# Expert jobs of 100 token slots instead of 128, and room for five overflow jobs, in a two-layer hybrid decoder trunk

## The chip, the cores and the metric

The kernel runs on one core of a Trainium2 chip. The metric is the device time of one execution in microseconds. Engines are named as in the profile: PE is the matrix engine and PEld its weight loads, DVE, ACT and POOL are the vector, scalar and general engines, SP is the engine that issues most DMAs. A matmul has a stationary operand, which is loaded into the array first, and a moving operand, whose columns stream through it.

## What is computed

The reference is a trunk of two layers on 256 tokens of width 1024, in float32. Each layer has a mixer (mLSTM heads and stick-breaking attention between one input and one output projection) and a channel mixer: a dense SwiGLU in layer 0, and in layer 1 eight experts of which every token takes two. The change concerns the experts:

```python
def _moe_swiglu(h, w_router, w_gate, w_up, w_down):
    logits = (h @ w_router).astype(jnp.float32)
    top_val, top_idx = lax.top_k(logits, TOP_K)           # TOP_K = 2, N_EXPERTS = 8
    top_w = jax.nn.softmax(top_val, axis=-1)
    combine = jnp.sum(jax.nn.one_hot(top_idx, N_EXPERTS) * top_w[..., None], axis=-2)
    out = jnp.zeros_like(h)
    for e in range(N_EXPERTS):
        out = out + combine[..., e:e + 1] * _swiglu(h, w_gate[e], w_up[e], w_down[e])
    return out
```

An expert's SwiGLU is `(silu(h @ w_gate) * (h @ w_up)) @ w_down`, with `w_gate` and `w_up` of 1024 x 3584 and `w_down` of 3584 x 1024. 256 tokens with two choices each make 512 pairs of token and expert, 64 for an expert on average. With the reference's own draw of inputs its router gives the eight experts 64, 79, 52, 85, 48, 84, 54 and 46 tokens.

## The kernel before

**Weights.** All weights stream from HBM in pieces of 1 MB (128 partitions x 2048 float32), through six buffers `raw`. Each piece is split on the chip into a high part `whi` (ACT, line 709) and a low part `wlo` (DVE, line 1169), with three buffers each. The products of float32 operands are made of three passes on PE (`passes`, line 1754): high x high, low activation x high weight, high activation x low weight. A piece takes 12 matmuls.

**Semaphores along a piece.** SP loads piece i when DVE has split piece i-6 (`lo_ready`); ACT splits piece i when PE has used piece i-3 (`piece_used`); DVE follows ACT; PE waits for `lo_ready`.

**Expert jobs.** A job is one expert on up to 128 tokens, in slots. It has 42 pieces: for each of seven blocks of 512 hidden columns two pieces of `w_gate`, two of `w_up` and two of `w_down`. In a job the tokens are the stationary operand (128 x 128: 128 features by 128 slots) and the weights move (512 columns). `product` makes gate and up into PSUM rows by slot, ACT and DVE form silu x up (lines 1052 and 1621), `hid_transpose` (line 2290) turns the 128 x 512 result in four transposes, ACT and DVE split it (lines 1058 and 1615), and `down_piece_job` multiplies with `w_down`. Eight jobs follow each other without a pause in PE's order: the next job's rows are fetched from `x_by_slot` by slot, turned in eight transposes (`gather`, line 2253) and split (lines 1040 and 1608) before the last down block of the job at hand. At the job's end ACT copies the result rows (line 1083) and sends them to `o_by_slot`. The first job gathers with matmuls against a one-hot matrix of slots (line 2240), the last adds its rows with a scatter matrix (lines 2324 to 2330), and the rows of the first seven are fetched back by an indirect gather (line 684) and added in the last job (line 1674).

**Overflow jobs.** Where an expert has more than 128 tokens, the rest goes to an overflow job, of which there may be `EXTRA = 3`. `count_extras` on DVE (the `ovf` lines in the diff) marks such experts and scans the marks; POOL makes from them a table with the expert of each overflow job and the count of all jobs (lines 666 to 679), in a chain of small operations, each waiting for the one before. At the end every engine loads the count and runs a loop of `EXTRA` rounds whose body is skipped when there is no such job (`Fori(E, JOBS)` and `If(j < jobs)`, on DVE lines 1730 to 1732, on PE lines 2373 to 2375).

**Routing, ahead of the jobs.** DVE makes the one-hot slots (line 1579) and the position of each token, POOL the rows for the indirect stores into `x_by_slot` (lines 615 to 630).

Of the kernel before, what the change touches and what calls it, by code (L numbers as in the profile page):

```python
# [63 lines left out]
EXTRA = 3  # L64
# [27 lines left out]
DUMP = E * P  # L92


def trunk(nc, x, w_in, b_igate, b_fgate, conv_w, conv_b, g_mlstm, g_sb, w_out,
# [4 lines left out]
    o_by_slot = nc.dram_tensor("o_by_slot", ((E - 1) * P, D), F32, kind="Internal").ap()  # L100
    with ExitStack() as ctx:
# [70 lines left out]
        table = sb("table", [P, 4])  # L172
        table_i = sb("table_i", [1, 4], I32)
# [42 lines left out]
        def first_rows(k):  # L216
            return ps[:, GATHER_BANK[k // 2], P * (k % 2):P * (k % 2 + 1)]
# [144 lines left out]
        def _(sp):  # L362
# [91 lines left out]
            def job(e, next_rows=False):  # L454
# [5 lines left out]
                for f in range(EB):  # L460
# [23 lines left out]
            jobs = sp.value_load(table_i[0:1, 3:4], min_val=E, max_val=JOBS)  # L484
# [18 lines left out]
        def _(pool):  # L503
# [82 lines left out]
            for e in range(1, E):  # L586
                pool.dma_start(x_by_slot[e * P:(e + 1) * P, :], vs[:].rearrange("p t d -> p (t d)")
                               ).then_inc(zero_rows, 16)
# [26 lines left out]
            routing_op(pool.tensor_scalar(where[:, 3, 0], iota_e[:], float(P), -1.0, ALU.mult, ALU.add))  # L615
            routing_op(pool.tensor_scalar(v, job_pos[:, :, 0:E], float(P), None, ALU.is_le))
# [46 lines left out]
            made, upto = ovf[:, 0], ovf[:, 1]  # L663
# [29 lines left out]
        def _(act):  # L693
# [342 lines left out]
            def gathered(o):  # L1036

                for half in range(2):
                    act.wait_ge(xg_ps, loop.at("half", 2 * o + half + 1))
                    act.activation(xT_hi[:, 4 * half:4 * half + 4, 0:P],  # L1040
                                   ps[:, 2 + half, :].rearrange("p (c t) -> p c t", t=P),
                                   ACT.Copy).then_inc(xg_hi_ready, 1)

            def scatter_matrix():
                act.wait_ge(scatT_ps, loop.at("job", 2 - E))
                act.activation(scatT[:], ps[:, 6, 0:256].rearrange("p (t c) -> p t c", t=TT),
                               ACT.Copy).then_inc(scatT_ready, 1)

            def e_silu(i, f):

                act.wait_ge(piece_used, loop.at("piece", n + i + 1))
                act.activation(silu[:, 0:512], ps[:, 2 * (f % 2), :], ACT.Silu).then_inc(e_sil, 1)

            def hid_high(f):
                act.wait_ge(e_hidT, loop.at("block", f + 1))
                if f >= 2:
                    act.wait_ge(piece_used, loop.at("piece", n + down_piece(f - 2, 1, EB) + 1))
                act.activation(hid_hi[:, f % 2, 0:512], ps[:, 4 + f % 2, :], ACT.Copy
                               ).then_inc(e_hid_hi, 1)
# [1365 lines left out]
```

## Time and profile before

| | |
|---|---|
| median of 3 runs | 1419.68 us (1419.65 to 1420.23) |
| profiled execution, its own time | 1420.34 us |
| its span | 1418.5 us |
| first matmul of the expert stage | 455.36 us |
| last weight matmul | 1406.56 us |

The span is that of the recorded instructions; the device time holds some 1.8 us around it. Matmuls overlap in the trace: each is shown with its whole passage through the array, and the next starts long before that ends. So the time that a matmul costs is read from the distance between starts. In the trace the three passes are named by their operands, moving first (`whi,xT_hi`, `whi,xT_lo`, `wlo,xT_hi`), and `128*100 128x256` means a stationary operand of 128 rows and 100 columns and a moving one of 256 columns.

### The profile page before, as it was taken

Reading aid. Unit: us, or ns where it says so; the run is one execution under the profiler, and the core shown is the slowest. Engines: PE = TensorE matmul, PEld = TensorE weight load, DVE = VectorE, ACT = ScalarE, POOL = GpSimd, SP = SyncE. Lnnn points to the kernel's source line nnn. Section 1 sums busy time; section 2 is a strip of 40 time slices with the busy share of each in tenths; the row PEclk is TensorE's granted clock in tenths of the full one; section 3 lists DMA queues with packets and bytes.
Section 4 is the critical chain, followed back from the end, with each engine's and each line's share of the span. In section 5 each row is a group of like instructions: output and inputs, shape, how many; then the busy total and the mean of one; then the engine's idle time right before and its main releaser. Section 6 shows DMA issues by size and latency. Waiting matters only on the chain.

```text
span 1418.5 us, 19026 instructions
## 1 busy us (share of the span) xinstructions
PE 1406.9 (99%) x7007; PEld 1185.5 (84%) x7007; DVE 1141.0 (80%) x854; ACT 1006.3 (71%) x866; POOL 161.4 (11%) x195
## 2 busy tenths in 40 slices
PE   9999999999999999999999999999999999999997
PEld 9988888889988888888888888888888888888885
DVE  6677554457587888888898988888888898888997
ACT  6877533445887777777777777777777777777775
POOL 2210000000101999500000000000000000002000
PEclk9999999999999999999999999999999999999999
DMA  9845655564544899999999999999999999999993
GB/s 352 268 153 191 215 198 178 176 195 152 183 149 144 325 394 397 392 395 385 364 383 393 370 380 392 382 369 390 382 361 385 392 370 380 382 389 376 394 394 135
DMA packets 188546, 447.04 MB, mean 315 GB/s; under 512 B 7736, under 2 KB 9920, under 8 KB 188496
## 3 DMA queue, kind: packets, MB, share of 16 engines
q1 hardware_dynamic: 184048, 431.12, 83.3%
q0 software_dynamic: 3440, 11.58, 2.2%
q10 hardware_dynamic: 1008, 3.67, 0.6%
q8 instruction: 32, 0.52, 0.2%
q14 instruction: 18, 0.15, 0.0%
HBM read 435.84 MB, written 10.49 MB: 315 GB/s over the span
## 4 chain that ended last, share of the span: by engine, by line
PE 97%; DVE 1%; ACT 1%; issue 0%; DMA 0%; SPq 0%; DVEq 0%; ACTq 0%
PE ps L1754 90%; PE ps L2290 2%; PE ps L2253 0%; PE ps L1786 0%; PE ps L1989 0%; PE ps L2113 0%; PE ps L1878 0%; DMA raw<-in_w_in_dram 0%; PE ps L2240 0%; ACT whi L709 0%; PE ps L1942 0%; PE ps L1775 0%; PE ps L1880 0%; DVE ssc L1380 0%; DVE y L1393 0%
## 5 line engine op out<-in xcount | busy, mean ns | idle before, releaser
L1169 DVE TENSOR_TENSOR wlo<-raw,whi 128x2048 fp32r<-128x2048 f32 x401 | 917.9, 2293 | 209.0 <-ACT whi L709 207.6
L709 ACT ACTIVATE whi<-raw 128x2048 fp32r<-128x2048 f32 x402 | 771.3, 1919 | 345.6 <-PE ps L1754 339.4
L1754 PE MATMUL ps<-whi,xT_hi 128*128 128x512 f32 (+1 forms) x1232 | 485.9, 394 | 0.3
L1754 PE MATMUL ps<-wlo,xT_hi 128*128 128x512 f32 (+1 forms) x1232 | 479.7, 389 | 0.0
L1754 PE MATMUL ps<-whi,xT_lo 128*128 128x512 f32 (+1 forms) x1232 | 478.8, 389 | 0.0
L1754 PEld LDWEIGHTS ps<-wlo,xT_hi 128*128 128x128 f32 x1232 | 231.2, 188 | 48.7
L1754 PEld LDWEIGHTS ps<-whi,xT_hi 128*128 128x128 f32 x1232 | 231.4, 188 | 46.6 <-issue 1.1
L1754 PEld LDWEIGHTS ps<-whi,xT_lo 128*128 128x128 f32 x1232 | 231.6, 188 | 44.9
L1754 PE MATMUL ps<-whi,hid_hi 128*128 128x512 f32 x536 | 210.2, 392 | 0.0
L1754 PE MATMUL ps<-wlo,hid_hi 128*128 128x512 f32 x536 | 208.8, 390 | 0.0
L1754 PE MATMUL ps<-whi,hid_lo 128*128 128x512 f32 x536 | 208.7, 389 | 0.0
L1754 PEld LDWEIGHTS ps<-wlo,hid_hi 128*128 128x128 f32 x536 | 100.6, 188 | 21.0
L1754 PEld LDWEIGHTS ps<-whi,hid_hi 128*128 128x128 f32 x536 | 100.7, 188 | 20.3
L1754 PEld LDWEIGHTS ps<-whi,hid_lo 128*128 128x128 f32 x536 | 100.7, 188 | 20.3
L684 POOL DMA_INDIRECT qsT<-o_by_slot,slot_out x1 | 1.8, 1792 | 707.9 <-DMA o_by_slot<-vm 707.9
L1754 PE MATMUL ps<-xT_hi,whi 128*128 128x256 f32 x252 | 72.3, 287 | 1.0 <-DVE wlo L1251 0.8
L1754 PE MATMUL ps<-xT_lo,whi 128*128 128x256 f32 x252 | 71.2, 283 | 0.0
L1754 PE MATMUL ps<-xT_hi,wlo 128*128 128x256 f32 x252 | 71.2, 283 | 0.0
L1754 PEld LDWEIGHTS ps<-xT_hi,whi 128*128 128x128 f32 x252 | 48.2, 191 | 2.0 <-issue 1.7
L1754 PEld LDWEIGHTS ps<-xT_lo,whi 128*128 128x128 f32 x252 | 48.3, 192 | 0.0
L1754 PEld LDWEIGHTS ps<-xT_hi,wlo 128*128 128x128 f32 x252 | 48.2, 191 | 0.0
L719 ACT ACT_TABLE_LOAD x32 | 41.1, 1283 | 1.3 <-PEq L2400 0.8
(286 smaller groups left out, 904.8 us busy)
## 6 DMA issues: line engine op xcount, KB each, us to landing
raw<-in_moe_w_gate_dram SPq DMA_DIRECT2D x112, 1024.0 KB, 7.2
raw<-in_moe_w_up_dram SPq DMA_DIRECT2D x112, 1024.0 KB, 7.3
raw<-in_moe_w_down_dram SPq DMA_DIRECT2D x112, 1024.0 KB, 7.3
raw<-in_w_in_dram SPq DMA_DIRECT2D x25, 1024.0 KB, 5.6
raw<-in_ffn_w_gate_dram SPq DMA_DIRECT2D x10, 1024.0 KB, 5.0
raw<-in_ffn_w_up_dram SPq DMA_DIRECT2D x10, 1024.0 KB, 5.1
raw<-in_ffn_w_down_dram SPq DMA_DIRECT2D x10, 1024.0 KB, 4.9
raw<-in_w_out_dram SPq DMA_DIRECT2D x8, 1024.0 KB, 5.1
```

Source lines behind the costliest of these rows:

```text
L684: pool.indirect_dma_start(picked[t][c], None, o_by_slot, bass.IndirectOffsetOnAxis(ap=slot_out[:, t, c:c + 1], axis=0)).then_inc(picked_in ...
L709: act.activation(whi[:, i % NSPLIT, :], raw[:, i % NRAW, :], ACT.Copy).then_inc(hi_ready, 1)
L719: act.preload_act_table_set(name)
L1169: dve.tensor_tensor(wlo[:, i % NSPLIT, :], raw[:, i % NRAW, :], whi[:, i % NSPLIT, :].bitcast(F32), ALU.subtract).then_inc(lo_ready, 1)
L1754: ins = pe.matmul(acc, lhs, rhs, start=start and m == 0, stop=stop and m == 2, skip_group_check=True)
L2290: ins = pe.transpose(ps[:, 4 + f % 2, k * P:(k + 1) * P], prod[:, k * P:(k + 1) * P], ident[:])
```

## The change

A job holds `SLOTS = 100` tokens instead of 128. Every operand of a job that had 128 slots has 100: the stationary operands of the products (`xT_hi`, `xT_lo`, `hid_hi`, `hid_lo`) have 100 columns, PSUM results and their evacuations that lie by slot in the partitions use 100 partitions, those that lie by slot in the free dimension are read as four groups of 100 columns out of 128 (`slot_columns`). The transposes read 100 rows and write 100 columns. `x_by_slot` and `o_by_slot` have 100 rows for each expert. An expert has one overflow job above 100 tokens and a second above 200; there may be five such jobs, so the skipped loops have five rounds. DVE counts them with one operation more, and POOL finds the expert of each by a range test in place of an equality, with two operations more for each overflow job and one ahead of them.

```diff
-EXTRA = 3
+SLOTS = 100
+EXTRA = 5
...
-DUMP = E * P
+DUMP = E * SLOTS
...
         def first_rows(k):
-            return ps[:, GATHER_BANK[k // 2], P * (k % 2):P * (k % 2 + 1)]
+            return ps[:, GATHER_BANK[k // 2], P * (k % 2):P * (k % 2) + SLOTS]
+
+        def slot_columns(v):
+
+            return v.rearrange("p (c t) -> p c t", t=P)[:, :, 0:SLOTS]
...
                         sp.wait_ge(xg_ps, loop.at("half", 2))
-                        sp.dma_start(x_slots, x_by_slot[bass.ds((e + 1) * P, P), :]
+                        sp.dma_start(x_slots[0:SLOTS], x_by_slot[bass.ds((e + 1) * SLOTS, SLOTS), :]
                                      ).then_inc(x_slots_in, 16)
...
+            table_op(pool.tensor_tensor(before, upto, before, ALU.subtract))
             for r in range(EXTRA):
-                table_op(pool.tensor_scalar(of, upto, float(r + 1), None, ALU.is_equal))
-                table_op(pool.tensor_tensor(of, of, made, ALU.mult))
+                table_op(pool.tensor_scalar(of, upto, float(r + 1), None, ALU.is_ge))
+                table_op(pool.tensor_scalar(names, before, float(r), None, ALU.is_le))
+                table_op(pool.tensor_tensor(of, of, names, ALU.mult))
                 table_op(pool.tensor_tensor(names, of, iota_e[:], ALU.mult))
                 sum_of(table[:, r:r + 1], names)
-                table_op(pool.tensor_scalar(back, of, -float(P), None, ALU.mult))
+                table_op(pool.tensor_scalar(back, before, float(SLOTS), -float((r + 1) * SLOTS),
+                                            ALU.mult, ALU.add))
+                table_op(pool.tensor_tensor(back, back, of, ALU.mult))
...
             def e_silu(i, f):
 
                 act.wait_ge(piece_used, loop.at("piece", n + i + 1))
-                act.activation(silu[:, 0:512], ps[:, 2 * (f % 2), :], ACT.Silu).then_inc(e_sil, 1)
+                act.activation(silu[0:SLOTS, 0:512], ps[0:SLOTS, 2 * (f % 2), :], ACT.Silu
+                               ).then_inc(e_sil, 1)
...
-                            act.activation(o_rows[:, c, :], ps[:, 6 + c, :], ACT.Copy
+                            act.activation(o_rows[0:SLOTS, c, :], ps[0:SLOTS, 6 + c, :], ACT.Copy
                                            ).then_inc((o_copied, o_free)[c], 1)
...
             def hid_low(f):
                 dve.wait_ge(e_hid_hi, loop.at("block", f + 1))
-                dve.tensor_tensor(hid_lo[:, f % 2, 0:512], ps[:, 4 + f % 2, :],
-                                  hid_hi[:, f % 2, 0:512].bitcast(F32), ALU.subtract
+                dve.tensor_tensor(slot_columns(hid_lo[:, f % 2, 0:512]), slot_columns(ps[:, 4 + f % 2, :]),
+                                  slot_columns(hid_hi[:, f % 2, 0:512].bitcast(F32)), ALU.subtract
                                   ).then_inc(e_hid, 1)
...
             def count_extras():
 
-                own(dve.tensor_scalar(ovf[:, 0], ps[:, 7, 16:24], float(P), None, ALU.is_gt))
+                own(dve.tensor_scalar(ovf[:, 2], ps[:, 7, 16:24], float(SLOTS), None, ALU.is_gt))
+                own(dve.scalar_tensor_tensor(ovf[:, 0], ps[:, 7, 16:24], float(2 * SLOTS), ovf[:, 2],
+                                             ALU.is_gt, ALU.add))
...
-                        ins = pe.transpose(ps[:, 2 + c // 4, P * (c % 4):P * (c % 4) + P],
-                                           x_slots[:, c * P:(c + 1) * P], ident[:])
+                        ins = pe.transpose(ps[:, 2 + c // 4, P * (c % 4):P * (c % 4) + SLOTS],
+                                           x_slots[0:SLOTS, c * P:(c + 1) * P],
+                                           ident[0:SLOTS, 0:SLOTS])
...
-                        ins = passes(ps[:, bank, :], xT_hi[:, kk, 0:P], xT_lo[:, kk, 0:P],
+                        ins = passes(ps[0:SLOTS, bank, :], xT_hi[:, kk, 0:SLOTS], xT_lo[:, kk, 0:SLOTS],
                                      hi[:, k, :], lo[:, k, :], start=half == 0 and k == 0,
                                      stop=half == 1 and k == 3, weights_move=True)
...
                 for k in range(4):
-                    ins = pe.transpose(ps[:, 4 + f % 2, k * P:(k + 1) * P],
-                                       prod[:, k * P:(k + 1) * P], ident[:])
+                    ins = pe.transpose(ps[:, 4 + f % 2, k * P:k * P + SLOTS],
+                                       prod[0:SLOTS, k * P:(k + 1) * P], ident[0:SLOTS, 0:SLOTS])
...
-                    hs = slice((2 * half + kk) * P, (2 * half + kk + 1) * P)
+                    hs = slice((2 * half + kk) * P, (2 * half + kk) * P + SLOTS)
                     s = slice(c * 512, (c + 1) * 512)
-                    ins = passes(ps[:, 6 + c, :], hid_hi[:, f % 2, hs], hid_lo[:, f % 2, hs],
+                    ins = passes(ps[0:SLOTS, 6 + c, :], hid_hi[:, f % 2, hs], hid_lo[:, f % 2, hs],
                                  hi[:, kk, s], lo[:, kk, s],
```

The other operands by slot are cut in the same way: the first gather and its copies, the splits of the gathered rows, the product, the scatter matrix, the last rows and their scatter.

## Rows read from the trace of the kernel before

**Rows 1.** The page, busy time of each engine.
```profile
PE 1406.9 (99%) x7007; PEld 1185.5 (84%) x7007; DVE 1141.0 (80%) x854; ACT 1006.3 (71%) x866; POOL 161.4 (11%) x195
```
**Rows 2.** Windows: us, busy by engine, PEclk, DMA share, GB/s; one job, then the stage.
```profile
808.39:926.92 118.53, 118.53 (x541) 98.14 (x540) 105.13 (x59) 89.37 (x60) 0.00 (x0) 1.00 1.02 380
...
459.05:1406.56 947.51, 947.51 (x4316) 784.31 (x4314) 842.84 (x486) 710.25 (x480) 128.85 (x134) 1.00 1.01 375
```
**Rows 3.** Waits from 573 to 1284 us: us in total, times, longest. The answer has five rows.
```profile
ACT whi L709 <- PE ps L1754: 164.1, 235, 0.9
DVE wlo L1169 <- ACT whi L709: 80.3, 192, 1.3
...
PEld ps L1754 <- DVE wlo L1169: 0.2, 1, 0.2
```
**Rows 4.** Timeline of PE, expert stage: start us, us, matmul; first and last of 12 distances.
```profile
799.75 0.39 PE L1754 MATMUL ps<-whi,xT_hi 128*128 128x512 f32 x1
...
802.47 0.39 PE L1754 MATMUL ps<-whi,hid_hi 128*128 128x512 f32 x1
```
**Rows 5.** Timeline of PEld, the same stretch.
```profile
800.20 0.19 PEld L1754 LDWEIGHTS ps<-whi,xT_hi 128*128 128x128 f32 x1
800.43 0.19 PEld L1754 LDWEIGHTS ps<-whi,xT_lo 128*128 128x128 f32 x1
```
**Rows 6.** Timeline of PE, mixer, 256 moving columns; first and last of 12 distances.
```profile
55.77 0.28 PE L1754 MATMUL ps<-xT_lo,whi 128*128 128x256 f32 x1
...
57.21 0.28 PE L1754 MATMUL ps<-xT_lo,whi 128*128 128x256 f32 x1
```
**Rows 7.** Timeline of PE, 384 moving columns; first and last of 7 distances.
```profile
293.93 0.33 PE L1754 MATMUL ps<-whi,xT_hi 128*128 128x384 f32 x1
...
295.14 0.33 PE L1754 MATMUL ps<-whi,xT_lo 128*128 128x384 f32 x1
```
**Rows 8.** Timeline of PE, gate products, 100 stationary columns; first and last of 14 distances.
```profile
24.61 0.28 PE L1942 MATMUL ps<-xT_lo,wif_hl 128*100 128x256 f32 x1
...
26.25 0.28 PE L1942 MATMUL ps<-xT_lo,wif_hl 128*100 128x256 f32 x1
```
**Rows 9.** Groups of PEld by form: busy us, mean ns, idle before.
```profile
L1754 PEld LDWEIGHTS ps<-whi,xT_hi 128*128 128x128 f32 x1232 | 231.4, 188 | 46.6 <-issue 1.1
...
L1942 PEld LDWEIGHTS ps<-xT_hi,wif_hl 128*100 128x100 f32 x16 | 2.7, 166 | 0.0
```
**Rows 10.** The chain, 800 to 830 us: start us, us, what.
```profile
808.55 0.87 PE ps L2253 x8
```
**Rows 11.** Timeline of ACT, DVE and PE from the end of one job into the next.
```profile
814.92 1.92 ACT L709 ACTIVATE whi<-raw 128x2048 fp32r<-128x2048 f32 x1 [0.80 <-PE ps L1754]
816.75 1.06 ACT L1083 ACTIVATE vm<-ps 128x512 f32<-128x512 f32 x2
818.43 3.85 ACT L709 ACTIVATE whi<-raw 128x2048 fp32r<-128x2048 f32 x2 [0.63 <-ACT vm L1083]
820.38 4.50 DVE L1169 TENSOR_TENSOR wlo<-raw,whi 128x2048 fp32r<-128x2048 f32 x2 [1.22 <-ACT whi L709]
822.89 0.40 PE L1754 MATMUL ps<-whi,xT_hi 128*128 128x512 f32 x1
```
**Rows 12.** The page, DMA issues: KB each, median us to landing.
```profile
raw<-in_moe_w_gate_dram SPq DMA_DIRECT2D x112, 1024.0 KB, 7.2
```
**Rows 13.** POOL: window of the table (us, busy), and its wait behind it.
```profile
514.48:590.29 75.81, 69.78 (x77) 1.00 1.04 395
POOL qsT L684 <- DMA o_by_slot<-vm: 707.9, 1, 707.9
```
**Rows 14.** DVE's skipped loop, by line: duration ns min/median/max, first and last start.
```profile
L1732 DVEq COMPARE_BRANCH  x3: 63/63/69, 1402.3 to 1404.1; - x3
L1731 DVEq COMPARE_BRANCH  x3: 50/66/72, 1403.0 to 1404.4; - x3
```
**Rows 15.** The end: chain (start us, us, what) and PE's skipped loop by line.
```profile
1406.25 0.70 DVE hid_lo L1627
...
1414.19 0.66 DVEq L101
L2375 PEldq COMPARE_BRANCH  x3: 221/221/3725, 1408.7 to 1413.8; - x3
```

More of the change, by code:

```diff
@@ L171, in trunk @@
         ovf = sb("ovf", [P, 8, E])
-        table = sb("table", [P, 4])
-        table_i = sb("table_i", [1, 4], I32)
+        table = sb("table", [P, EXTRA + 1])
+        table_i = sb("table_i", [1, EXTRA + 1], I32)
         slot_in = sb("slot_in", [P, TT, 2], I32)
@@ L483, in _ @@
             sp.wait_ge(table_ready, 1)
-            jobs = sp.value_load(table_i[0:1, 3:4], min_val=E, max_val=JOBS)
+            jobs = sp.value_load(table_i[0:1, EXTRA:EXTRA + 1], min_val=E, max_val=JOBS)
             with sp.Fori(E, JOBS) as j:
@@ L614, in _ @@
             pool.wait_ge(picked_second, 1)
-            routing_op(pool.tensor_scalar(where[:, 3, 0], iota_e[:], float(P), -1.0, ALU.mult, ALU.add))
-            routing_op(pool.tensor_scalar(v, job_pos[:, :, 0:E], float(P), None, ALU.is_le))
+            routing_op(pool.tensor_scalar(where[:, 3, 0], iota_e[:], float(SLOTS), -1.0, ALU.mult,
+                                          ALU.add))
+            routing_op(pool.tensor_scalar(v, job_pos[:, :, 0:E], float(SLOTS), None, ALU.is_le))
             for t in range(TT):
@@ L1100, in rows_of_job_behind @@
                         act.wait_ge(piece_used, loop.at("piece", n))
-                    act.activation((o_hi, o_plain)[c], ps[:, 6 + c, :], ACT.Copy).then_inc(o_hi_ready, 1)
+                    act.activation((o_hi, o_plain)[c][0:SLOTS], ps[0:SLOTS, 6 + c, :], ACT.Copy
+                                   ).then_inc(o_hi_ready, 1)
             def start_of_job(first=False):
@@ L1108, in start_of_job @@
                             act.wait_ge((xg_first, xg_ps)[k // 2 % 2], k // 4 + 1)
-                        act.activation(xT_hi[:, k, 0:P], first_rows(k), ACT.Copy,
+                        act.activation(xT_hi[:, k, 0:SLOTS], first_rows(k), ACT.Copy,
                                        scale=gT[:, ROUTE_SEAM, k:k + 1]).then_inc(xg_first_hi, 1)
@@ L1125, in _ @@
             act.wait_ge(table_ready, 1)
-            jobs = act.value_load(table_i[0:1, 3:4], min_val=E, max_val=JOBS)
+            jobs = act.value_load(table_i[0:1, EXTRA:EXTRA + 1], min_val=E, max_val=JOBS)
             with act.Fori(E, JOBS) as j:
@@ L1600, in one_hot @@
                         else job_pos[:, t, (0, E - 1)[o]:(1, E)[o]]
-                    dve.tensor_scalar(slots[:, t, :], iota[:], at, None, ALU.is_equal
+                    dve.tensor_scalar(slots[:, t, 0:SLOTS], iota[:, 0:SLOTS], at, None, ALU.is_equal
                                       ).then_inc(slots_ready, 1)
@@ L1729, in _ @@
             dve.wait_ge(table_ready, 1)
-            jobs = dve.value_load(table_i[0:1, 3:4], min_val=E, max_val=JOBS)
+            jobs = dve.value_load(table_i[0:1, EXTRA:EXTRA + 1], min_val=E, max_val=JOBS)
             with dve.Fori(E, JOBS) as j:
@@ L2239, in first_gather @@
                     for c in range(KC):
-                        ins = pe.matmul(first_rows(c), h[:, t, c * P:(c + 1) * P], slots[:, t, :],
+                        ins = pe.matmul(first_rows(c), h[:, t, c * P:(c + 1) * P], slots[:, t, 0:SLOTS],
                                         start=t == 0 and c % 2 == 0, stop=t == 1, skip_group_check=True)
@@ L2263, in scatter_matrix @@
                 for t in range(TT):
-                    ins = pe.transpose(ps[:, 6, t * P:(t + 1) * P], slots[:, t, :], ident[:])
+                    ins = pe.transpose(ps[0:SLOTS, 6, t * P:(t + 1) * P], slots[:, t, 0:SLOTS], ident[:])
                 ins.then_inc(scatT_ps, 1)
@@ L2323, in scatter @@
                     bank = ps[:, 2 + 2 * t, :]
-                    pe.matmul(bank, scatT[:, t, :], o_hi, start=True, stop=False,
+                    pe.matmul(bank, scatT[0:SLOTS, t, :], o_hi[0:SLOTS], start=True, stop=False,
                               skip_group_check=True)
-                    pe.matmul(bank, scatT[:, t, :], o_lo, start=False, stop=True,
+                    pe.matmul(bank, scatT[0:SLOTS, t, :], o_lo[0:SLOTS], start=False, stop=True,
                               skip_group_check=True).then_inc(scat_ps, 1)
@@ L2329, in scatter @@
                 for t in range(TT):
-                    pe.matmul(ps[:, 3 + 2 * t, :], scatT[:, t, :].bitcast(F32), o_plain, start=True,
-                              stop=True, skip_group_check=True).then_inc(scat_ps, 1)
+                    pe.matmul(ps[:, 3 + 2 * t, :], scatT[0:SLOTS, t, :].bitcast(F32), o_plain[0:SLOTS],
+                              start=True, stop=True, skip_group_check=True).then_inc(scat_ps, 1)
             def start_of_job(first=False):
@@ L2372, in _ @@
             pe.wait_ge(table_ready, 1)
-            jobs = pe.value_load(table_i[0:1, 3:4], min_val=E, max_val=JOBS)
+            jobs = pe.value_load(table_i[0:1, EXTRA:EXTRA + 1], min_val=E, max_val=JOBS)
             with pe.Fori(E, JOBS) as j:
```

39 lines of the change are left out of this document (19 added, 20 removed).

## The prediction

> **What bounds the kernel now.** I read the page first: PE is busy for 99% of the span, but a busy share of overlapping matmuls says only that PE is never empty, and DVE is at 80% [rows 1]. So the question is whether PE is fed all the time. The windows show one job of 118.53 us with PE full, DVE busy for 105.1 us (89%) and ACT for 89.4 us, the clock at its full level and 380 GB/s moving; the expert stage is 947.5 us, two thirds of the span [rows 2]. The waits of that stage then tell who is late: ACT waits for PE to free a split buffer (164 us), DVE waits for ACT, and PE waited for DVE once, for 0.2 us [rows 3]. The stage is bound by PE alone, and each nanosecond between two starts of its matmuls counts.
>
> What is that distance? In a product of a job 12 distances take 802.47 - 799.75 = 2.72 us, so 226.7 ns each for 512 moving columns [rows 4]. In the mixer, with the same 128 stationary columns, 12 distances take 1.44 us for 256 moving columns: 120.0 ns [rows 6]; with 384, 7 distances take 1.21 us: 173 ns [rows 7]. From 256 to 512 columns the distance grows by 106.7 ns, 0.417 ns a column, one column per cycle at 2.4 GHz. What is left is the same at all three lengths: 226.7 - 213.3 = 13.4, 173 - 160 = 13, 120.0 - 106.7 = 13.3 ns. So every matmul pays a fixed 13.3 ns that its moving columns do not explain. It isn't the wait for the weight load: the load for the next matmul begins with the present one (800.20, 800.43) and takes 0.19 us, so it is done some 35 ns before the next start [rows 4, 5].
>
> As a check on a job: 8 x 42 pieces x 12 matmuls are 4032 in the stage, 504 in a job. 504 x 0.2267 = 114.3 us. A job has 28 + 8 transposes; eight of them are 0.87 us, 0.109 us each [rows 10], so 36 are 3.9 us. Together 118.2 us of the 118.53 measured [rows 2]. Nothing large is missing.
>
> **The change, part by part.**
>
> *The stationary operand of 4032 matmuls has 100 columns instead of 128.* The trace has one place with this shape: the gate products of the mixer at L1942, in the same number format, with 256 moving columns. Their 14 distances take 26.25 - 24.61 = 1.64 us, 117.1 ns each [rows 8], against 120.0 ns with 128 stationary columns [rows 6]. The fixed part is then 117.1 - 106.7 = 10.4 ns, and 13.3 x 100/128 = 10.4 ns: it goes by the stationary columns, 0.104 ns for each. As the fixed part didn't depend on the moving length, I take the difference of 2.9 ns over to 512 columns: 226.7 becomes 223.8 ns. Rounding of the starts (0.01 us in 14 and in 12) leaves 0.7 to 0.8 ns on each distance, so 2.9 is between some 2 and 4. The sum: 4032 x 2.9 ns = 11.7 us, with 8.1 and 16 us at these ends. The bounds from both sides: no gain if the difference of L1942 has another cause; at most the whole fixed part, 4032 x 13.3 ns = 54 us. I take 11.7 because both rows differ in the stationary columns and in nothing else that I can see. The loads become shorter too, 188 to 166 ns [rows 9]; they lie beside the matmul, so I count that at nothing.
>
> The Trainium skill (TensorE: Matmul & The Clock Gate, section Back-to-back issue gap) gives the warm gap of an isolated matmul as N/2.4 + 2.5 ns, with N the moving columns and no term for the stationary ones; that is an estimate of 216 ns here. The rows have 226.7 ns [rows 4], and two distances at one N that differ by 2.9 ns [rows 6, 8]; by the rule the change would bring nothing from PE, which is the first rival below.
>
> *Transposes and first gather.* In a transpose the data are the stationary operand, with 128 columns as before; only the identity, which moves, shrinks from 128 to 100 columns. Their distance of 109 ns [rows 10] is twice the 53 ns that 128 columns stream, so something else sets it (the load, it seems) and 100 columns bring nothing. The same holds for the first gather. The final scatter keeps 128 stationary and 512 moving columns and has 100 rows instead of 128, which I price at nothing: it is eight matmuls.
>
> *ACT and DVE.* Copies and subtractions that lie by slot in the free dimension have 400 elements per partition instead of 512, and are shorter; those that lie by slot in the partitions still have 512 and should keep their time. None is on PE's path as long as pieces arrive in time. The place with least cover is the seam between jobs. ACT splits a piece (from 814.92), copies the result rows (816.75, two of them), sends them and splits again (818.43, two pieces); DVE follows with the second at 820.38 + 2.29 = 822.67, and PE starts that piece at 822.89 [rows 11]. The cover is 0.22 us. No operation of this chain becomes shorter (splits of 2048, copies of 512 elements), while PE's 36 matmuls of three pieces become 36 x 2.9 ns = 0.10 us shorter. So 0.12 us are left. If that fell short, each seam would pay the shortfall, seven times; if all cover of 0.22 us had to be paid on top, 1.5 us. I put 0.1 us for it, as it is thin.
>
> *Weight DMAs.* A piece of 1 MB lands 7.2 us after its issue [rows 12]. It is issued when DVE has split the piece six before, and needed when ACT starts on it, six pieces of 2.82 us (118.53/42) less 1.92 + 2.29 us later: 12.7 us. That leaves 5.5 us, of which the change takes 0.2. The rate rises from 380 to 380 x 118.5/117.1 = 385 GB/s, and the window of the table shows 395 [rows 13]. Price nothing. The row stores and loads become smaller.
>
> *POOL's table.* The chain had 77 operations in 75.81 us [rows 13], 0.985 us each. It was 25 for each of three jobs and two behind; it becomes 27 for each of five, one ahead and two behind: 138, so 61 more, 60 us. Queued behind it on POOL is the indirect gather of the result rows, which waits 707.9 us for the seventh job's store [rows 13]; the four engines that load the table do so at the end. The cover is ten times the cost. Without it the last job's additions would be late. The one operation more on DVE lies in the first job, where DVE has its 11% of slack [rows 2].
>
> *Skipped loops.* Two rounds more on each engine. On DVE the branches of three rounds run from 1402.3 to 1404.4, 0.7 us a round [rows 14]; two more end at about 1405.8. DVE's next operation starts at 1406.25 [rows 15], released by ACT, which waits for PE: 0.4 us of cover, and nothing to pay. If DVE's rounds were dearer, up to 1.4 us would stand in the path; I put 0.1 us. PE's loop starts at 1408.7 behind its last work and its third round begins at 1413.8, with a first branch of 3.7 us; two rounds at 0.7 us end near 1415.6, after DVE's last work but before the last stores are in, at 1418.5 [rows 15]. ACT waits for PE's last piece at that time, SP for DVE's last rows; both have microseconds.
>
> **Sum.** -11.7 + 0.1 + 0.1 = -11.5 us. The profiled execution took 1420.34 us with a span of 1418.5, so its span would become 1407.0. The median of the runs before is 1419.68 us, 0.7 below the profiled execution, and the difference goes on it: 1419.7 - 11.5 = 1408.2 us.
>
> **Rivals.**
> 1. *The matmuls don't speed up.* The distance at 512 moving columns stays at 226.7 ns, because the 2.9 ns of L1942 belong to short matmuls or to a quieter stretch (only 14 distances in a row). Against it: the fixed part was one value at 256, 384 and 512 [rows 4, 6, 7]. Time: 1419.7 + 0.2 = 1419.9 us, so this is also the case that the change doesn't do anything measurable.
> 2. *PE gains, but the splits hold it back.* At 89% of a job DVE is near to PE, and the seam has 0.12 us. If strided operands made the slot operations longer instead of shorter, so that each seam lost 0.3 us and each of 56 blocks 0.05 us, 7 x 0.3 + 56 x 0.05 = 4.9 us would come back: 1413 us.
> 3. *Slower: a ninth job runs.* It starts with the 101st token of any expert, costs a whole job of 118.5 us and some 10 us of unhidden gather and scatter at both ends, and gives 1408.2 + 128 = 1536 us. Against it: before there were exactly 8 jobs (112 gate pieces, 14 a job) [rows 12], so no expert has over 128, and the largest count of the reference's draw is 85.
> 4. *More than the share.* Loads shorter by 22 ns [rows 9] could relieve PE beyond the fixed part's share; half of the 13.3 ns would be 27 us, 1393 us.
> 5. *Loads become longer.* If loads were on a fast path that only 128 columns have, they would at 100 take perhaps twice as long, 376 ns, and set the distance: +150 ns x 4032 = +600 us, 2020 us. The 166 ns of L1942's loads speak against it [rows 9].
>
> The Trainium skill (TensorE: Matmul & The Clock Gate, section Weight-path perf modes) has such a path: fast weight load is on when the number of weights is 128 and the type isn't FP32. By the loads of 188 and 166 ns, in the proportion of a fixed time and the columns, it isn't in use here.
>
> **Chances.** Forecast 0.76, with 1406.5 to 1410.5 as its own range; rival 1 0.11; rival 2 0.06; rival 3 0.04; rival 4 0.02; rival 5 0.01. A measurement of this kernel tells 0.2% (2.8 us) from no change. Faster: 0.76 + 0.06 + 0.02 = 0.84. Same: 0.11. Slower: 0.05. The range takes in the forecast and rival 2, 0.82 together: 1405.5 to 1414 us.
>
> **What the profile after would show.** Distances of 223.8 ns in the products of a job and a job of 118.53 - 504 x 0.0029 = 117.1 us; loads of 166 ns; transposes still 109 ns apart; no new wait of PE for DVE; 112 gate pieces; POOL's table ending near 650 us; DVE's loop done before 1395 (1405.8 - 11.5 is 1394.3) and its next operation when ACT releases it. Distances of 226.7 ns would prove me wrong at the root; distances of 223.8 with a job of over 117.5 us would show the splits or seams.

## The result and the profile after

| | before | after |
|---|---|---|
| median | 1419.66 us | 1437.26 us |
| span of the profiled execution | 1418.5 us | 1435.9 us |

The changed kernel is slower: the ratio is 1.0123, with a 95% interval of 1.0111 to 1.0135. The forecast was 1408.2 us, faster.

The page of the changed kernel, busy time of the engines and its groups (busy us, mean ns, idle before); compare [rows 1, 9]:

```profile
PE 1424.5 (99%) x7007; PEld 1087.8 (76%) x7007; DVE 1133.3 (79%) x855; ACT 999.0 (70%) x866; POOL 206.6 (14%) x256
...
L1768 PE MATMUL ps<-whi,xT_hi 128*100 128x512 f32 (+2 forms) x1232 | 489.2, 397 | 0.7 <-DVE wlo L1182 0.4
...
L1768 PEld LDWEIGHTS ps<-whi,hid_lo 128*100 128x100 f32 (+1 forms) x536 | 90.3, 168 | 33.1
...
raw<-in_moe_w_gate_dram SPq DMA_DIRECT2D x112, 1024.0 KB, 7.2
```

As many matmuls as before, 112 gate pieces, so eight jobs and no overflow job. PE still has no pause, its loads became shorter, DVE and ACT have less to do, and it takes longer. The windows of one job and of the stage (us, busy of PE, PEld, DVE, ACT, POOL, granted clock, DMA share, GB/s), to be read against [rows 2]:

```profile
815.31:935.97 120.66, 120.66 (x542) 85.85 (x541) 104.11 (x59) 88.48 (x60) 0.00 (x0) 1.00 1.02 372
459.05:1424.19 965.14, 964.76 (x4315) 685.94 (x4314) 834.58 (x486) 702.99 (x480) 174.18 (x195) 1.00 1.00 367
```

A job takes 120.66 us instead of 118.53: 8 x 2.13 = 17.0 of the 17.4 us by which the span grew. The clock is at its full level in both. The timeline of PE from a gate and up product into a down piece (start us, us, matmul), first and last of 20 distances, answers to [rows 4]:

```profile
805.87 0.40 PE L1768 MATMUL ps<-whi,xT_hi 128*100 128x512 f32 x1
...
810.54 0.40 PE L1768 MATMUL ps<-wlo,hid_hi 128*100 128x512 f32 x1
```

4.67 us for 20 distances are 233.5 ns, against 226.7 ns before. The transposes went the other way. The chain of the changed kernel (start us, us, what), against [rows 10]:

```profile
815.47 0.69 PE ps L2267 x8
```

0.086 us each, from 0.109. The two together give the job: before, (118.53 - 36 x 0.109) / 504 = 227.4 ns on average for a product's matmul, some distances being stretched; after, (120.66 - 36 x 0.086) / 504 = 233.3 ns. So the matmuls cost 4032 x 5.9 ns = 23.8 us and the transposes give back 0.023 us each; there are 8 x 28 in the hidden blocks and 7 x 8 in the gathers, as the first job gathers with matmuls, so that is 280 x 0.023 = 6.4 us. The balance is 17.4 us.

The waits of the stage hold a second, small thing (us in total, times, longest):

```profile
ACT whi L721 <- DMA raw<-in_moe_w_gate_dram: 3.3, 2, 2.5
...
PEld ps L1768 <- DVE wlo L1182: 1.1, 2, 0.8
```

ACT waited for weight DMAs, which before it didn't, in the stretch of [rows 3] or in the rest of the stage, and PE once for its split, for 0.55 us beyond a normal distance.

### The profile page after: what moved, and what is told of

It is laid out like the page before. It is cut to its first block, busy times and chain, and to the rows that moved or that the text cites. A ratio compares the mean times of both kernels' runs of the same rounds, so it can differ in the third digit from the quotient of the medians.

```text
span 1435.9 us, 19120 instructions
## 1 busy us (share of the span) xinstructions
PE 1424.5 (99%) x7007; PEld 1087.8 (76%) x7007; DVE 1133.3 (79%) x855; ACT 999.0 (70%) x866; POOL 206.6 (14%) x256
## 4 chain that ended last, share of the span: by engine, by line
PE 94%; DVE 2%; DMA 2%; ACT 1%; issue 1%; SPq 0%; DVEq 0%; ACTq 0%
PE ps L1768 88%; PE ps L2305 1%; DMA raw<-in_moe_w_gate_dram 1%; DMA h<-in_x_dram 1%; ACT whi L721 1%; DVE wlo L1182 1%; PE ps L1800 0%; PE ps L2003 0%; PE ps L2127 0%; PE ps L2267 0%; PE ps L1892 0%; ACT y L746 0%; PE ps L2254 0%; SPq L412 0%; PE ps L1789 0%
## 5 line engine op out<-in xcount | busy, mean ns | idle before, releaser
L1768 PE MATMUL ps<-whi,xT_hi 128*100 128x512 f32 (+2 forms) x1232 | 489.2, 397 | 0.7 <-DVE wlo L1182 0.4
L1768 PE MATMUL ps<-wlo,xT_hi 128*100 128x512 f32 (+2 forms) x1232 | 483.9, 393 | 0.0
L1768 PE MATMUL ps<-whi,xT_lo 128*100 128x512 f32 (+2 forms) x1232 | 483.9, 393 | 0.0
L1768 PEld LDWEIGHTS ps<-wlo,xT_hi 128*100 128x100 f32 (+1 forms) x1232 | 210.5, 171 | 74.2
L1768 PEld LDWEIGHTS ps<-whi,xT_hi 128*100 128x100 f32 (+1 forms) x1232 | 210.6, 171 | 72.0 <-issue 1.1
L1768 PEld LDWEIGHTS ps<-whi,xT_lo 128*100 128x100 f32 (+1 forms) x1232 | 210.7, 171 | 69.5
L1768 PE MATMUL ps<-whi,hid_hi 128*100 128x512 f32 (+1 forms) x536 | 212.4, 396 | 0.0
L1768 PE MATMUL ps<-whi,hid_lo 128*100 128x512 f32 (+1 forms) x536 | 211.2, 394 | 0.0
L1768 PE MATMUL ps<-wlo,hid_hi 128*100 128x512 f32 (+1 forms) x536 | 211.2, 394 | 0.0
L1768 PEld LDWEIGHTS ps<-whi,hid_hi 128*100 128x100 f32 (+1 forms) x536 | 90.3, 168 | 33.2
L696 POOL DMA_INDIRECT qsT<-o_by_slot,slot_out x1 | 2.9, 2883 | 676.2 <-DMA o_by_slot<-vm 676.2
```

Source lines behind the costliest of these rows:

```text
L696: pool.indirect_dma_start(picked[t][c], None, o_by_slot, bass.IndirectOffsetOnAxis(ap=slot_out[:, t, c:c + 1], axis=0)).then_inc(picked_in ...
L1768: ins = pe.matmul(acc, lhs, rhs, start=start and m == 0, stop=stop and m == 2, skip_group_check=True)
```

## The experiments

The question was why a matmul with 100 stationary columns takes 233.3 ns here, when the same width at L1942 had looked cheap. I started with two theories: **WIDTH**, such a matmul is slower by itself; **SURROUNDINGS**, it is slowed by what ACT, DVE, the DMAs or the rest of the change do. **FORM** and **PHASE** came later, as told below. Distances in the tables are worked out from the starts of the matmuls in each trace, once they are steady: the first few of a block, which can be up to 0.32 us, are left out.

**Blocks of matmuls in a quiet stretch.** Behind the last work of the kernel before:

```diff
+            pe.wait_ge(job_done, E + 1)
+            for kr, n, m in PROBES:
+                for r in range(30):
+                    pe.matmul(ps[0:m, r % 2, 0:n], xT_hi[0:kr, r % 8, 0:m], whi[0:kr, r % 3, 0:n],
+                              start=True, stop=True, skip_group_check=True)
```

> The kernel before, with 16 blocks of 30 matmuls behind PE's last work, when DVE, ACT and the DMA queues are nearly done; every matmul has its own weight load, and the blocks differ in stationary columns (64 to 128), moving columns (256, 384, 512) and rows (128, 100). Theory WIDTH: a matmul of 100 stationary and 512 moving columns takes 233 ns by itself, whatever goes on around it; then the block 128*100 128x512 shows 233 ns and the block 128*128 128x512 shows 226.6 ns. Theory SURROUNDINGS: the 233 ns of the changed kernel come from what ACT, DVE and the DMAs do beside it or from its strided operands; then the 100-column block shows some 223.8 ns in this quiet stretch. With 256 moving columns both expect 120 ns for 128 and 117 ns for 100 stationary columns, as in the mixer. The other widths (64, 80, 96, 104, 112, 120, 124) are there to see by what steps the distance goes.

| stationary x moving columns | ns | | ns |
|---|---|---|---|
| 128 x 512 (last block) | 227.1 | 100 x 512 | 226.7 |
| 124 x 512 | 228.3 | 120 x 512 | 233.4 |
| 112 x 512 | 233.3 | 104 x 512 | 229.0 |
| 96 x 512 | 230.1 | 80 x 512 | 233.4 |
| 64 x 512 | 230.0 | 128 x 512, 100 rows | 226.9 |
| 128 x 384 | 173.3 | 100 x 384 | 173.1 |
| 128 x 256 | 120.1 | 100 x 256 | 117.8 |
| 96 x 256 | 116.0 | | |

WIDTH in its plain form fell: 100 x 512 ran at 226.7 ns. But the 223.8 ns of the other theory, which was also my forecast, did not appear either. No width was faster than 128 columns by more than 0.4 ns with 512 moving columns, and there is no order in the values, 124 and 104 near 229, 120 and 112 at 233. The difference that L1942 had shown is there with 256 moving columns (2.3 ns), is 0.2 ns with 384 and has no successor with 512.

**The parts of the change.** Three kernels tell the operands from the rest. The first sets the width back and keeps table and loops:

```diff
-SLOTS = 100
+SLOTS = 128
```

> The changed kernel with SLOTS = 128: the table of five overflow jobs, the longer POOL chain, the additional DVE operation and the five skipped rounds stay, the operands have 128 slots again. If the loss comes from the operands (both theories), this takes what the kernel before takes, 1419.7 us within 1 us. If table or loops cost anything, it is above that by their share of the 17.6 us.

1419.97 us, ratio to the kernel before 0.9997 (0.9988 to 1.0007). Table, POOL chain, DVE operation and skipped rounds cost nothing that could be measured.

The second keeps everything but the stationary width of the products:

```diff
-                        ins = passes(ps[0:SLOTS, bank, :], xT_hi[:, kk, 0:SLOTS], xT_lo[:, kk, 0:SLOTS],
+                        ins = passes(ps[:, bank, :], xT_hi[:, kk, 0:P], xT_lo[:, kk, 0:P],
...
-                    hs = slice((2 * half + kk) * P, (2 * half + kk) * P + SLOTS)
+                    hs = slice((2 * half + kk) * P, (2 * half + kk + 1) * P)
```

> The changed kernel with one part undone: the stationary operands of the three products of a job have 128 columns again (the 28 behind the slots hold leftovers that are not used), and the splits of the hidden block are contiguous again. Rows, transposes, table and loops stay as changed. WIDTH: the distance in products is 226.6 ns again, the transposes keep their 85 ns instead of 109, which saves 8 x 36 x 0.0235 = 6.8 us: 1419.7 - 6.8 = 1413 us. SURROUNDINGS (the rest of the change disturbs PE): the distance stays near 233 ns and the time near 1437 us.

1415.36 us, ratio 0.9966 (0.9954 to 0.9977), faster than before. Its windows (columns as above):

```profile
808.21:925.94 117.73, 117.73 (x541) 97.54 (x540) 104.91 (x59) 89.18 (x60) 0.00 (x0) 1.00 1.03 383
```

A job takes 117.73 us: 0.80 less than before, the 36 transposes at 0.023 us. The 28 unused columns are worth 120.66 - 117.73 = 2.93 us a job. So the whole loss sits in the stationary width of the products. The 2.4 us by which it missed the expected 1413 us are taken up below.

The third asks for the role of the number 100:

```diff
-SLOTS = 100
+SLOTS = 96
```

> The changed kernel with SLOTS = 96, all else the same (no expert has more than 85 tokens, so eight jobs run). If the distance goes smoothly with the width, 96 lies beside 100: some 233 ns, 1437 us. If 100 is dear because it is no multiple of 32, the distance has its fixed part in proportion, 213.3 + 13.3 x 96/128 = 223.3 ns: 4032 x 3.3 = 13 us less than before, transposes of 96 moving columns at 0.85 ns a column save 8 x 36 x 27 ns = 7.8 us: 1399 us.

1423.50 us, ratio 1.0025 (1.0015 to 1.0035). Neither expectation held. Its job takes 118.98 us, with product distances of 230 ns, the value of the 96-column block above. 96, a multiple of 32, is not fast either.

**Form, surroundings or phase.** In the quiet stretch 100 x 512 had come directly behind a block of 128 x 512. In a job it comes behind transposes, adds up in one PSUM bank and turns between high and low parts. The next blocks tell these apart; each is set off by four short matmuls:

```diff
+            def as_jobs(m, count=36):
+                for r in range(count):
+                    x, w = ((xT_hi, whi), (xT_lo, whi), (xT_hi, wlo))[r % 3]
+                    pe.matmul(ps[0:m, 0, :], x[:, r // 3 % 8, 0:m], w[:, 0, 512 * (r // 3 % 4):512 * (r // 3 % 4) + 512],
+                              start=r == 0, stop=r == count - 1, skip_group_check=True)
...
+            mark(); as_jobs(P)
+            as_jobs(100)
```

> The kernel before, with other blocks of 36 matmuls of 512 moving columns in the quiet stretch behind PE's last work, each block set off by four short matmuls. With 100 stationary columns: writing to two PSUM banks in turn (226.7 ns in the first probe run); adding up in one bank; turning between xT_hi, xT_lo, whi and wlo; and both, as in a job. Then the job form for 128, 96, 112, 120, 124, 104, 64 and 32 columns, and 100 columns directly behind 128 without a break. Theory FORM: what makes 233 ns of 226.7 is the form of a job, adding up in one bank or the turn of operands; then one of these blocks at 100 shows 233 ns. Theory SURROUNDINGS: all of them show 226.7 ns or less, since ACT, DVE and DMA rest. Theory PHASE: the distance at widths other than 128 depends on how the block begins; then the 100-column blocks differ among each other without order, and the one directly behind 128 columns stays at 226.7 ns.

| block, 512 moving columns | ns |
|---|---|
| 100, two banks in turn | 233.4 |
| 100, one bank | 233.3 |
| 100, operands in turn | 233.4 |
| 100, as in a job | 233.4 |
| 100, as in a job, directly behind 36 of 128 | 226.7 |
| 128, as in a job | 227.0 |
| 96, 112, 120 | 230.2, 229.2, 233.3 |
| 124, 104, 64, 32 | 228.5, 228.9, 229.8, 231.7 |

The first of these is the very form that had run at 226.7 ns in the run before. FORM fell, and SURROUNDINGS too as the only cause, since 233 ns appear here with ACT, DVE and DMA at rest. PHASE had let expect that the blocks of 100 columns differ among each other; the four behind short matmuls didn't, only the one behind wide ones did. What differs between the two values of 100 columns is only what stood ahead. The turn from 128 to 100 columns in this trace (timeline of PE), with no step in the distance:

```profile
1476.37 0.39 PE L2407 MATMUL ps<-whi,xT_lo 128*128 128x512 f32 x1
1476.60 0.39 PE L2407 MATMUL ps<-wlo,xT_hi 128*128 128x512 f32 x1
1476.83 0.39 PE L2407 MATMUL ps<-whi,xT_hi 128*100 128x512 f32 x1
...
1484.76 0.39 PE L2407 MATMUL ps<-wlo,xT_hi 128*100 128x512 f32 x1
```

35 distances from 1476.83 to 1484.76 are 226.6 ns each.

Surroundings were taken away from the job itself, in two ways:

```diff
-                act.activation(whi[:, i % NSPLIT, :], raw[:, i % NRAW, :], ACT.Copy
+                z = 256 if i >= MOE_BASE + 3 else PIECE
+                act.activation(whi[:, i % NSPLIT, 0:z], raw[:, i % NRAW, 0:z], ACT.Copy
```

> The changed kernel, whose splits on ACT and DVE in the expert jobs cover 256 of 2048 columns (the rest of each piece is left unsplit, so this part of the computation is left out); PE's instructions, the loads and their order stay. SURROUNDINGS by ACT or DVE: the distance in jobs falls from 233.3 ns towards 227 or below, and the expert stage is some 25 us shorter, 1410 us. FORM or PHASE: it stays at 233.3 ns, some 1437 us.

```diff
+                if i >= MOE_BASE + NRAW:
+                    rows_ = w[half * 512:half * 512 + P, bass.ds(c0, n)]
+                    load(i, [(v[:, 0:1], rows_.rearrange("(k p) n -> p k n", p=P))])
+                    return
```

> The changed kernel, whose loads in the expert jobs bring a quarter of each piece (the rest of the weights is left out of the computation); ACT, DVE and PE do the same instructions as in the changed kernel. SURROUNDINGS by DMA writes: the distance falls from 233.3 ns towards 227 or below, and the time towards 1410 us. FORM or PHASE: it stays at 233.3 ns and 1437 us.

The same window of the two kernels, short splits first:

```profile
815.31:935.97 120.66, 120.66 (x543) 85.85 (x542) 27.15 (x58) 25.79 (x60) 0.00 (x0) 1.00 1.02 372
```

```profile
815.31:935.97 120.66, 120.66 (x543) 85.85 (x542) 104.12 (x59) 88.51 (x61) 0.00 (x0) 1.00 0.44 137
```

DVE busy for 27 us instead of 104, and DMA at 137 GB/s instead of 372: the job stays at 120.66 us in both, and the times are 1437.12 and 1437.16 us. Neither ACT and DVE nor the loads make the 233 ns; each was taken away by itself, and in the blocks above all of them rested. PE loses this time within itself.

**Phase, in the quiet stretch.** Blocks of 36 matmuls of 100 x 512 behind different leads:

```diff
+            for lead in (1, 2, 3, 4, 6, 12):
+                mark()
+                as_jobs(P, lead)
+                as_jobs(100)
+            for m in (100, P):
+                mark()
+                as_jobs(P, 12)
+                turns(m)
+                as_jobs(100)
```

> The kernel before, with blocks of 512 moving columns in the quiet stretch behind PE's last work. PHASE: 36 matmuls of 100 columns behind 1, 2, 3, 4, 6 and 12 of 128 columns, after four short matmuls, run at 226.7 ns from some lead on and at 233.3 ns below it; 36 directly behind four transposes run at 233.3 ns, as in the jobs of the changed kernel, also where 12 wide matmuls stand ahead of the transposes; 1, 2, 3, 5 or 7 short matmuls ahead may give either value; 120 behind 12 wide ones stay at 226.7 ns to the end. FORM: no block differs by what stands ahead of it.

| ahead of the block of 100 columns | ns |
|---|---|
| four short, then 1, 2, 4 or 6 wide | 233.3, 233.4, 233.3, 233.3 |
| four short, then 3 or 12 wide | 226.7, 226.7 |
| four transposes, 100 or 128 moving columns | 233.3, 233.2 |
| 12 wide, then four transposes of either kind | 233.3, 233.3 |
| 1, 2, 5 short | 233.1, 233.4, 233.4 |
| 3, 7 short | 226.7, 226.7 |
| 12 wide, block of 120 | 226.7 |

Two of these blocks in the timeline of PE, behind two wide matmuls and behind three; the dots stand for the inside of a block:

```profile
1441.59 0.39 PE L2395 MATMUL ps<-whi,xT_lo 128*128 128x512 f32 x1
1441.82 0.40 PE L2395 MATMUL ps<-whi,xT_hi 128*100 128x512 f32 x1
...
1449.99 0.40 PE L2395 MATMUL ps<-wlo,xT_hi 128*100 128x512 f32 x1
...
1451.14 0.39 PE L2395 MATMUL ps<-wlo,xT_hi 128*128 128x512 f32 x1
1451.37 0.39 PE L2395 MATMUL ps<-whi,xT_hi 128*100 128x512 f32 x1
...
1459.31 0.39 PE L2395 MATMUL ps<-wlo,xT_hi 128*100 128x512 f32 x1
```

35 distances take 8.17 us (233.4 ns) in the first and 7.94 us (226.9 ns, to the rounding) in the second. The same 36 instructions run in one of two steady rhythms, 544 or 560 cycles at 2.4 GHz, and which one is settled within the first few of them. Once in a rhythm they stay: 120 of them in the fast one, from 1579.91 to 1606.88. It did not become steady from "some lead on", as I had expected; 3 wide ones led to the fast rhythm, 4 and 6 to the slow one. Blocks of 128 columns begin with distances like 228, 232 and 231 ns and are back at 226.7 ns within a dozen, whatever stands ahead. Behind transposes the 100-column blocks took the slow rhythm in all four tries, and in a job every stretch of products begins behind transposes.

**Phase, in the jobs.** The decisive run: wide operands only in the first stretch behind each group of transposes.

```diff
+                        m = (P, SLOTS)[half]
-                        ins = passes(ps[0:SLOTS, bank, :], xT_hi[:, kk, 0:SLOTS], xT_lo[:, kk, 0:SLOTS],
+                        ins = passes(ps[0:m, bank, :], xT_hi[:, kk, 0:m], xT_lo[:, kk, 0:m],
...
+                    m = P if (f, half) in ((EB - 2, 1), (EB - 1, 0)) else SLOTS
```

> The changed kernel, in which only the first stretch behind each group of transposes is wide: the first 12 matmuls of every product of two pieces, and the one down piece behind the last transposes and behind the gather, have 128 stationary columns; the other 312 of a job's 504 keep 100. Theory PHASE (a 100-column matmul keeps the rhythm in which its stretch began; 128 columns always find back to 226.7 ns): all distances are about 226.7 ns, and the time is that of the kernel with 128 stationary columns throughout, 1415.4 us. Theory FORM (100 columns cost 233.3 ns where they stand, wide ones 226.7): 8 x 312 x 6.6 ns = 16.5 us more, 1432 us.

1415.63 us, ratio 0.9969 (0.9956 to 0.9981): PHASE's 1415.4, not FORM's 1432. The timeline of PE where a product goes from its wide half to its narrow one:

```profile
819.03 0.39 PE L1768 MATMUL ps<-wlo,xT_hi 128*128 128x512 f32 x1
819.26 0.39 PE L1768 MATMUL ps<-whi,xT_hi 128*100 128x512 f32 x1
819.49 0.39 PE L1768 MATMUL ps<-whi,xT_lo 128*100 128x512 f32 x1
...
821.98 0.39 PE L1768 MATMUL ps<-whi,xT_hi 128*128 128x512 f32 x1
```

12 distances of narrow matmuls take 2.72 us, 226.7 ns each, in the middle of a job. The stage has 120 such stretches of narrow matmuls, and 113 of them run so. The other seven, of 12 matmuls each, ran at 233 ns although wide ones stood directly ahead. One (526.53 us) began while the wide ones ahead had not yet settled. The other six are the narrow half of the first up product behind a seam, in six of the seven jobs that have a seam ahead. At the third seam:

```profile
824.47 0.39 PE L1768 MATMUL ps<-wlo,xT_hi 128*128 128x512 f32 x1
824.70 0.40 PE L1768 MATMUL ps<-whi,xT_hi 128*100 128x512 f32 x1
...
827.27 0.40 PE L1768 MATMUL ps<-wlo,xT_hi 128*100 128x512 f32 x1
```

11 distances from 824.70 take 2.57 us, 233.6 ns each. In the next job the same 11 take 945.03 - 942.54 = 2.49 us, at 226.7 ns to the rounding. At this place PE takes up a piece right when DVE has split it. In the six jobs the last distance ahead of the stretch is 228 to 382 ns and the first within it 234 to 313, in that one they are 226 and 227; so it seems that a start late by a few ns is enough for the slow rhythm, which no run tests by itself. That is PHASE once more, in a job and with the same instructions, but it also says that settled wide matmuls ahead don't make the fast rhythm certain. These seven stretches cost 77 x 6.7 ns = 0.5 us of the profiled execution. That execution was the longest of the six (1418.61 us; the others took 1415.3 to 1416.2), for another reason: in the first job PE waited for the late weight piece of the next paragraph, with 2.21 us between two starts at 519.87 us, and then the clock fell to its lower level (us, busy of PE, granted clock, DMA share, GB/s):

```profile
522.60:525.80 3.20, 3.20 (x9) 0.50 1.04 409
```

Seven distances there are 427 ns.

**The late weight piece.** In the kernel with 128 stationary columns the longest distance between two starts of the stage was 1.97 us, near 520 us, where 0.23 are normal, and the granted clock stayed at its full level; in the changed kernel it was 0.78 us at the same place. The chain of the changed kernel there (start us, us, what):

```profile
503.49 14.24 DMA raw<-in_moe_w_gate_dram
```

The piece came after 14.24 us. The windows in which the first row load comes in (issued at 501 us, behind weight pieces in the queue), before and after (the last two numbers are DMA share and GB/s):

```profile
509.00:514.00 5.00, 5.00 (x26) 4.14 (x24) 4.57 (x3) 4.42 (x4) 4.72 (x4) 1.00 1.04 391
```

```profile
509.00:514.00 5.00, 5.00 (x26) 3.61 (x25) 4.07 (x2) 3.77 (x5) 4.64 (x5) 1.00 1.04 261
```

The rate falls from 391 to 261 GB/s while the DMA engines show as busy. It does so at each of the seven row loads, below 320 GB/s for 3 to 7 us, in the kernels with 100 and with 96 rows; behind the first there is little cover. In the first job pieces landed after some 12 us even before, it seems because the queues are still full from the indirect row stores. To test the row load alone, in the kernel with 128 stationary columns (the zeroing of the last expert's rows grows to 128 rows with it):

```diff
-                        sp.dma_start(x_slots[0:SLOTS], x_by_slot[bass.ds((e + 1) * SLOTS, SLOTS), :]
+                        sp.dma_start(x_slots, x_by_slot[bass.ds((e + 1) * SLOTS, P), :]
```

> The kernel with 128 stationary columns in the products (1415.4 us), whose row loads from x_by_slot bring 128 rows instead of 100 into 128 partitions; only 100 are used. In the changed kernels the load rate falls from 388 to some 260-280 GB/s for 4 us behind each such row load, and in the first job a weight piece came 14 us after its issue, for which PE waited 1.7 us in that kernel. If the load to 100 partitions is the cause, the rate stays at 388 GB/s, the wait goes and the time is 1413.7 us. If it is not (another address, other rows in HBM), both stay and the time is 1415.4 us.

1414.25 us, ratio 0.9959 (0.9945 to 0.9973), the fastest kernel of this study; that it beats the one without this edit (0.9966) isn't shown by these intervals. The mechanism is shown by its windows:

```profile
509.00:514.00 5.00, 5.00 (x26) 4.18 (x25) 4.40 (x3) 4.79 (x4) 4.64 (x5) 1.00 1.03 392
```

392 GB/s with more bytes moved and the same first address of each row load, and no wait of PE is left at this place; 0.4 us remain in the second job. With SLOTS = 96 the rate in this window was 261 GB/s as well. So a row load to 96 or 100 partitions slows itself and the traffic beside it for some 4 us (it took 9.0 us from issue to landing with 96 rows, in the median, and 6.9 here), and one to 128 doesn't. What happens in the DMA engines isn't settled by this.

## Why the prediction was wrong

**The step that failed.** "As the fixed part didn't depend on the moving length, I take the difference of 2.9 ns over to 512 columns." The distance of 128 columns is stream plus a constant at 256, 384 and 512 [rows 4, 6, 7]; I had one length only for 100 columns [rows 8], and took for granted that it keeps the same law. It doesn't: 117.8 ns at 256, 173.1 at 384 (0.2 less than 128 columns), 226.7 or 233.3 at 512. The term sized at -11.7 us came out at +23.8 us (4032 x 5.9 ns). The agreement of 13.3 x 100/128 with 10.4 I let stand as a law; in the quiet blocks it isn't exact even at 256 moving columns, where 100 stationary ones take 117.8 ns (the law has 117.1) and 96 take 116.0 (116.7). The check I could have made on paper was that 117.1 ns, in a stretch of 14 distances, is also 0.457 ns a column, which at 512 gives 234 ns; one point can't choose between a smaller constant and a dearer column. Neither is the law: at 384 they give 170.4 and 175.7, and 173.1 was measured. That 226.7 ns became 233.3 in the jobs, and not only stayed, is the rhythm in which stretches behind transposes start; what makes it inside PE is open.

**The bounds.** I bounded this unknown by "no gain" and "the whole fixed part", so a loss from the width was in no case of mine, although nothing in the trace excluded it. The price of a shape that the trace doesn't hold, 100 by 512, needed an end below zero. The rivals on the slow side were a ninth job, which didn't run, and weight loads of twice the length, which became shorter. The rule of the Trainium skill (TensorE: Matmul & The Clock Gate, section Back-to-back issue gap), which gives the gap of an isolated matmul by the moving columns alone, was nearer than my sum: at 128 columns its estimate of 216 ns stays 11 below the measured 226.7, and it has no room for two rhythms, but it would not have promised a gain.

**Transposes.** "100 columns bring nothing" was wrong in the other direction: 0.109 to 0.086 us is 0.85 or 0.86 ns for each moving column at 128, 100, and 96 (0.082). I saw that 109 ns is twice the stream and named the load; it is the stream itself, two cycles a column. Rows and moving columns shrank together in the transposes, but the last scatter's plain float32 matmuls of 512 moving columns, four at the end of the stage, tell them apart: 428 to 429 ns from one to the next with 128 rows and with 100, at the full clock, again two cycles a column and nothing by rows. For the first gather I was right that 100 columns bring nothing: its matmuls are 111 to 112 ns apart with 128 and with 100 moving columns. The transposes were 6.4 us of gain that I left out, and the reason why the kernels with wide products beat the one before.

**Weight DMAs.** Priced at nothing, with a rate of 385 GB/s. The rate was no limit, but the row load to 100 partitions was, for 4 to 6 us at each of the seven. The 5.5 us of cover came from the median landing of 7.2 us; in the first job pieces landed after some 12 us already before, so there it was 12.7 - 12 = 0.7 us. It cost PE 0.55 us in the changed kernel, 1.7 in the one whose PE is faster, and more where the clock fell behind it. "The row stores and loads become smaller" was true in bytes and wrong in time.

**Right.** Table, POOL chain and skipped loops cost nothing, as the run with 128 slots shows; POOL's last gather waited 676.2 us instead of 707.9. DVE's loop of five rounds ended at 1423.2 and its next operation began at 1423.86, with cover. The loads fell to the 164 to 166 ns of [rows 9] and gave PE nothing.

**The seam.** Its cover was read too large: the matmul at 822.89 [rows 11] was preceded by its weight load, which in that trace began at 822.73, 0.06 us after the split and 0.08 us later than its neighbours do, and the distance ahead was already 235 ns. So the cover was nothing, and each seam already cost some 0.05 us in distances a few ns too long. This wasn't put to the test in the changed kernel, since PE became slower; in the kernel with wide products PE waited for a split by more than such an amount only in the first two jobs.

## What to carry to other kernels

Read the distance between matmul starts, and price a new shape only from that very shape: a stationary width and a moving length together. Narrower stationary operands bought nothing with 512 moving columns in any width tried, and at 100 and 112 columns the distance hung on what ran before; leave unused columns in the operand and cut the moving side instead, as the transposes show. When a DMA is cut to fewer partitions, look at the rate around it, not at its bytes. And judge the cover of a transfer by the slowest stretch that it has to cover, not by the median.

## What the runs showed of the hardware

- A stream of matmuls, each with its own load, with 512 moving columns and 100 stationary ones, has two steady rhythms, 226.7 and 233.3 ns (544 and 560 cycles). The same instructions take either, by what stands ahead. 128 columns settle at 226.7 ns from any start that was tried. 112 columns too showed two values, 233.3 and 229.2 ns. In a job, directly behind twelve settled matmuls of 128 columns, the same stretch took the slow rhythm five times and the fast one once. What in PE makes the rhythm is open.
- Transposes of float32 take 0.85 ns for each moving column, with 128 columns being the stationary side; plain float32 matmuls of 512 moving columns are 428 to 429 ns apart, with 128 rows or 100.
- Matmuls of 128 stationary columns, each with its own load, are 111 to 112 ns apart with 64 moving columns (the short ones ahead of the blocks).
- The traffic around a row load to 96 or 100 partitions ran at 261 GB/s instead of 391, for some 4 us.
- PE waited for some 5 us ahead of the blocks in the quiet stretch. The next matmuls of 128 x 512 were 427 ns apart, at the lower of the two clock levels (the window from 1410 to 1420 us has a mean granted clock of 0.83), and then 226.7 ns. Inside the stage the clock fell to the lower level once, behind a pause of PE of 2.0 us (519.87 to 522.08 us in the kernel with wide first stretches).
